# One DiT step on a Trainium2 core: half of the modulation moved from TensorE to VectorE multiply-adds

## The reference

```python
mod = silu(cond) @ w_mod + b_mod          # -> sh1, sc1, g1, sh2, sc2, g2, 2048 columns each
h = x * (1 + sc1) + sh1
z = h @ w_in                              # 8 neighbourhood heads (NA), latents of 8 MLA heads
o = concat(neighbourhood attention, latent attention) @ w_o
x = layernorm(ALPHA * x + g1 * o)
y = layernorm(ALPHA * x + g2 * swiglu(x * (1 + sc2) + sh2))
```

## Time and profile before

| | |
|---|---|
| median of 3 runs | 3181.38 us (3173.12 to 3184.36) |
| the profiled execution | 3185.31 us, span 3183.8 us, 43487 instructions |
| TensorE busy | 3027.6 us (95%), 16238 matmuls |
| weight loads | 2545.2 us (80%), beside the matmuls |
| VectorE busy | 1712.4 us (54%) |
| ScalarE busy | 1184.1 us (37%) |
| GpSimd busy | 168.1 us (5%) |
| split, VectorE L1202 | 239 recorded, 290.6 us, mean 1230 ns |
| split, ScalarE L752 | 239 recorded, 246.0 us, mean 1056 ns |
| load of a stream block | 503 of 512 KB, median 3.5 us from issue to landing |
| DMA over the span | 380 MB, 119 GB/s |

### The profile page before, as it was taken

The page is one execution under the profiler, slowest core; times in us unless marked ns, Lnnn a source line. Parts: engine busy times, 40 slices in busy tenths (PEclk is TensorE's granted clock), DMA queues, the critical chain, the costliest instruction groups (busy, mean ns, idle before and its releaser), DMA issues.

```text
span 3183.8 us, 43487 instructions
## 1 busy us (share of the span) xinstructions
PE 3027.6 (95%) x16238; PEld 2545.2 (80%) x16238; DVE 1712.4 (54%) x2513; ACT 1184.1 (37%) x1966; POOL 168.1 (5%) x203
## 2 busy tenths in 40 slices
PE   7899999999999999959999999999999999899997
PEld 2587676677766577849999999999999877687885
DVE  7626566551333432276666666666666534433348
ACT  7425555442433421164444444444444311212121
POOL 0200101000000010000000000000000000000004
PEclk9899999999989999969999999999999999999998
DMA  9836555641120131122222222222222423323232
GB/s 371 268 107 223 188 198 189 199 150 68 46 95 33 45 119 67 60 93 101 93 103 105 95 92 105 98 98 96 102 94 105 158 88 127 111 89 115 88 108 84
DMA packets 103745, 379.99 MB, mean 119 GB/s; under 512 B 13153, under 2 KB 13370, under 8 KB 102106
## 3 DMA queue, kind: packets, MB, share of 16 engines
q1 hardware_dynamic: 89088, 317.36, 28.0%
q0 software_dynamic: 13840, 61.02, 5.6%
q10 hardware_dynamic: 730, 0.38, 0.1%
HBM read 347.09 MB, written 35.31 MB: 120 GB/s over the span
## 4 chain that ended last, share of the span: by engine, by line
PE 82%; DVE 7%; DMA 5%; issue 3%; ACT 3%; SPq 0%; ACTq 0%; DVEq 0%; POOL 0%; POOLq 0%
PE ps L1682 13%; PE ps L1684 13%; PE ps L1683 13%; PE ps L2123 11%; PE ps L2125 11%; PE ps L2124 11%; DMA raw<-in_wstream 3%; PE ps L1853 2%; DVE wlo L1202 1%; DMA mraw<-in_wstream 1%; ACT whi L752 1%; PE ps L1805 1%; PE ps L1804 1%; PE ps L1826 1%; DVE mlo L1217 1%
## 5 line engine op out<-in xcount | busy, mean ns | idle before, releaser
L2123 PE MATMUL ps<-acth,ringh 128*128 128x320 f32 x2464 | 762.8, 310 | 17.4 <-DVE ringl L1507 17.4
L2124 PE MATMUL ps<-actl,ringh 128*128 128x320 f32 x2464 | 762.5, 309 | 0.0
L2125 PE MATMUL ps<-acth,ringl 128*128 128x320 f32 x2464 | 762.4, 309 | 0.0
L1202 DVE TENSOR_TENSOR wlo<-raw,whi 128x1024 fp32r<-128x1024 f32 x239 | 290.6, 1230 | 496.7 <-ACT whi L752 496.5
L2123 PEld LDWEIGHTS ps<-acth,ringh 128*128 128x128 f32 x2464 | 463.2, 188 | 17.8 <-DVE ringl L1507 17.8
L2124 PEld LDWEIGHTS ps<-actl,ringh 128*128 128x128 f32 x2464 | 463.2, 188 | 0.0
L2125 PEld LDWEIGHTS ps<-acth,ringl 128*128 128x128 f32 x2464 | 463.2, 188 | 0.0
L752 ACT ACTIVATE whi<-raw 128x1024 fp32r<-128x1024 f32 x239 | 246.0, 1056 | 402.0 <-PE ps L1684 374.7
L1682 PE MATMUL ps<-dwh,fring 128*128 128x512 f32 x820 | 327.3, 399 | 23.3 <-DVE dwl L1594 18.5
L1683 PE MATMUL ps<-dwl,fring 128*128 128x512 f32 x820 | 324.5, 396 | 0.0
L1684 PE MATMUL ps<-dwh,fring 128*128 128x512 f32 x820 | 324.5, 396 | 0.0
(11 more groups left out here) (294 smaller groups left out, 4907.0 us busy)
## 6 DMA issues: line engine op xcount, KB each, us to landing
raw<-in_wstream SPq DMA_DIRECT2D x503, 512.0 KB, 3.5
mraw<-in_wstream SPq DMA_DIRECT2D x64, 512.0 KB, 7.6
fscr<-fst POOLq DMA_DIRECT2D x44, 320.0 KB, 2.4
fst<-fscr SPq DMA_DIRECT2D x21, 640.0 KB, 4.1
acc<-in_xT SPq DMA_DIRECT2D x8, 640.0 KB, 18.8
oscr<-ost POOLq DMA_DIRECT2D x16, 320.0 KB, 2.5
acc<-in_xtok POOLq DMA_DIRECT2D x1, 5120.0 KB, 16.1
ostage<-oscr POOLq DMA_DIRECT2D x16, 320.0 KB, 3.9
```

The costliest lines, as they stand in the source:

```text
L1202: V.tensor_tensor(lo_of(n), raw[:, n % 4, :], hi_of(n).bitcast(f32), ALU.subtract).then_inc(lo_ready, 1)
L2123: mm(out, ringh[:, s, w], ah, start=first, stop=False, skip_group_check=True)
L2124: mm(out, ringh[:, s, w], al, start=False, stop=False, skip_group_check=True)
L2125: ins = mm(out, ringl[:, s, w], ah, start=False, stop=last, skip_group_check=True)
```

## The change

The first half of the modulation, and all that is not the modulation, computes what it did. The 128 blocks of the second half are no longer split and no longer go to TensorE. VectorE multiplies each by the conditioning as a per-partition scalar and adds it up, 128 x 512 at a time, for two rows and two halves of the block: four instructions. What is left is a sum over the 128 partitions, which TensorE does once per chunk, as rows (`row_sums`, for the gates) or as columns (`column_sums`, for shift2 and scale2). The gates get their bias on VectorE (`gate_row`), go to DRAM and are spread to 128 partitions by DMA.

```diff
+            def gemv(i, m, part=(0, 1)):
+                nb, u = MOD_SEQ.index(m), m // 8
+                s, b, buf = slot_of("m", m), m % 8, macc_of(u)
+                for kk in part:
+                    w = raw[:, s, kk * 512:(kk + 1) * 512]
...
+                    for c in range(2):
+                        if kk:
+                            dve.wait_ge(m_half, at(i, 8, 2 * nb + c + 1))
...
+                        v = buf[:, c, :]
...
+                            ins = V.scalar_tensor_tensor(out=v, in0=w, scalar=f, in1=v, op0=ALU.mult, op1=ALU.add)
...
+            def gate_row(u, bank):
+                dve.wait_ge(mred, reduces(u if u < 4 else u + 8))
+                dve.wait_ge(brow_in, 16 * (u + 1))
+                V.tensor_tensor(grow[:, :], ps[bank][0:2, :], grow[:, :], ALU.add).then_inc(grow_ready, 1)
...
+            def row_sums(u, bank):
+                pe.wait_ge(lo_ready, POS[("m", 8 * u + 7)] + 1)
+                mm(ps[bank][0:2, :], unit[:, 1:3], macc_of(u)[:, 0, :], start=True, stop=False)
+                mm(ps[bank][0:2, :], unit[:, 0:2], macc_of(u)[:, 1, :], start=False, stop=True).then_inc(mred, 1)
...
+            def column_sums(units, bank):
+                for n, u in enumerate(units):
...
+                    for j in range(4):
...
+                        mm(o, macc_of(u)[:, 0, w], unit[:, 1:3], start=True, stop=False)
+                        ins = mm(o, macc_of(u)[:, 1, w], unit[:, 0:2], start=False, stop=True)
```

The 128 blocks are placed over five stages instead of one:

```diff
+V_MODS = [0] * 4 + [1] * 8 + [2] * 4
+WO_MODS = [0 if b < 4 or b > 26 else 2 if 9 <= b < 18 else 1 for b in range(32)]
...
+    for h in range(NH):
+        order += [("m", 64 + 4 * h), ("m", 65 + 4 * h), ("w", B_HEAD + h + 2), ("m", 66 + 4 * h), ("m", 67 + 4 * h)]
```

That is 16 in the V projection, 32 in the NA stage (four per head, in halves between the softmax stages), 16 in the latent projections (one per block), 32 in the MLA heads (four per head) and 32 in the output projection (blocks 4 to 26). SyncE's loads are written out one by one in this order. In the NA stage and in the heads VectorE's queue becomes:

```diff
             def na_iter(i, stages):
+                for g in range(4):
+                    if stages:
+                        stage(i, -1, 2 * g, True, (1,))
+                        stage(i, -1, 2 * g, True, (0,))
+                    gemv(i, 32 + 8 * g, (0,))
+                    if g == 3:
+                        k_copy(at(i, 4, B_NA + 4), HT)
+                    split(i, B_NA + g + 2)
+                    if stages:
+                        stage(i, -1, 2 * g + 1, True, (1,))
+                        stage(i, -1, 2 * g + 1, True, (0,))
+                    elif g in (0, 3):
+                        gate_row(g // 3, 6 - g // 3)
+                    gemv(i, 32 + 8 * g, (1,))
...
                 if h < NH:
+                    if h == 0:
+                        dve.wait_ge(skv_out, 32)
+                    gemv(None, 64 + 4 * h)
+                    gemv(None, 65 + 4 * h)
 
                     dve.wait_ge(used, B_HEAD + h + 1)
                     V.tensor_copy(kT[:, 0:KEYS // 2], ps[0][:, 0:KEYS // 2]).then_inc(k_evac, 1)
                     for s in range(5):
                         stage(None, NH + h, s, False)
                         if s == 1:
-                            split(None, 0, B_HEAD + h + 2)
+                            split(None, B_HEAD + h + 2)
+                        if s in (2, 3):
+                            gemv(None, 64 + 4 * h + s)
```

On TensorE the feature block of the NA stage is cut in two (`outs=(0, 1)` and `(2, 3)`) with a `stage` call after each half. Row sums stand after V block 13, in the first NA head, after latent blocks 9 and 16 and four times in the output projection; column sums of shift2 in the first latent block, those of scale2 after block 0 of the output projection. Ahead of the NA loop TensorE waits for the second gate row:

```diff
             na_iter(None, False)
+
+            pe.wait_ge(grow_ready, 2)
+            pe.wait_ge(v_evac, 2 * TT)
             with pe.Fori(1, NH) as i:
...
+                if b == 0:
+                    column_sums(range(8, 12), 6)
+                if b in WO_ROWS:
+                    u = WO_ROWS.index(b)
+                    if u >= 2:
+                        pe.wait_ge(grow_ready, 3 + u)
+                    row_sums(12 + u, 4 + u % 2)
```

In the output projection VectorE's multiply-adds follow the split of each block, those of b = 7, 15 and 23 the evacuation of that block; GpSimd's queue gets the gate broadcast and the load of xs, which moves there from the first MLA head:

```diff
                 if k == 3:
-                    rows_in(rows2, D, 2 * D, rows2_in)
...
+                    pool.wait_ge(grow_out, 64)
+                    for c in range(2):
+                        pool.dma_start(gate[:, c, :], modg[c:c + 1, 0:D].to_broadcast([P, D])).then_inc(gate_in, 16)
+                if k == 8:
+                    pool.wait_ge(mred, reduces(11))
+                    pool.dma_start(xs, xtok).then_inc(xs_in, 16)
```

More of the change, by code:

```diff
@@ L485, in _, with stream_load @@
                 if g < 4:
[L486 to L494, removed]
+                    sp.dma_start(raw[:, g, :], wstream[stream_row(B_V + g)]).then_inc(loaded[g], 16)
+            def stream_load(p):
+                sp.wait_ge(lo_ready, p - 3)
+                sp.dma_start(raw[:, p % 4, :], wstream[stream_row(p)]).then_inc(loaded[p % 4], 16)
+            for p in range(B_V + 4, len(ORDER)):
+                stream_load(p)
             def gu_load(i, jj):
@@ L499, in gu_load @@
                         if q < 2:
-                            sp.wait_ge(lo_ready, B_FF - 2 + q)
+                            sp.wait_ge(lo_ready, max(p for p in range(len(ORDER)) if p % 4 == q) + 1)
                         if q == 2:
@@ L1259, in _ @@
                         h_rest(k)
-                        if b == 0 and 0 < k < 4:
-                            split(None, 0, B_V + k)
-                split(None, 0, B_V + b + 4)
+                        if b == 0 and k == 1:
+                            split(None, B_V + 1)
+                split(None, B_V + b + 2)
+                m = sum(V_MODS[:b])
+                for x in range(V_MODS[b]):
+                    gemv(None, m + x)
             def stage(i, a, s, na, parts=(0, 1)):
@@ L1466, in _ @@
                 if b < 30:
-                    split(None, 0, B_WO + b + 2)
-                if b == 24:
+                    split(None, B_WO + b + 2)
+                m = 96 + sum(WO_MODS[:b])
+                for x in range(WO_MODS[b]):
+                    gemv(None, m + x)
+                if b in WO_ROWS:
+                    gate_row(4 + WO_ROWS.index(b), 4 + WO_ROWS.index(b) % 2)
+                if b == 2:
                     mod2_parts()
@@ L1702, in tok_block, with feat_block @@
                 return ins
-            def feat_block(n, bh, bl, k0, first, last, before=None, after=None, widths=(HT, HT), banks=(0, 1, 2, 3), b2=None):
-                for o in range(4):
+            def feat_block(n, bh, bl, k0, first, last, before=None, after=None, widths=(HT, HT), banks=(0, 1, 2, 3), b2=None,
+                           outs=range(4)):
+                for o in outs:
                     if before:
@@ L1756, in _ @@
             turn_rows(None, 7)
-            def mod_columns(shift, scale, done):
-                for j in range(2 * KD):
-                    rows = shift if j < KD else scale
-                    ins = mm(ps[6][:, 2 * j:2 * j + 2], rows[:, j % KD * P:(j % KD + 1) * P], selt[:, 0:2],
-                             start=True, stop=True)
-                ins.then_inc(done, 1)
             for c in range(2):
```

449 lines of the change are left out of this document (240 added, 209 removed).

## The result

The changed kernel takes 3095.6 us (3082.4 to 3096.8, four runs) where the kernel before takes 3178.8: a ratio of 0.973, interval 0.970 to 0.976. The forecast was 3138 us. The kernel became faster, as forecast, and the heads behaved as told; the gain is 83 us instead of 43, about twice as large.

The account below looks back on a forecast made before the run. TensorE, busy in 95% of the span, was taken as the bound, stage by stage. From 3185.3 us: -4.5 - 7.6 - 7.1 - 120 + 17 + 80.5 + 6.7 - 8.2 = -43.2, less 3.9, gives 3138; range 3076 to 3172.

Parts of the forecast that it names:

- Heads: MLA heads: four multiply-add blocks each delay the kT copy, TensorE pauses and its clock falls; +80.5 us.
- The half clock: MLA heads: after the pause, scores and part of the PV product go at half clock; 7.5 us per head, seven times.
- The late kT: MLA heads: kT copy ends late behind multiply-adds, so TensorE stops for 3.5 us in each of eight heads.
- NA loop: Seven NA iterations: modulation products and idle time go, 58.4 to 41.3 us each; -120 us, bounds -127 and -100.
- meetings with GpSimd: NA loop: 1 us added per iteration, 40.3 to 41.3 us.
- rival C: NA iteration becomes bound by softmax and multiply-add chain; at 46 us it gives back 33, total 3171 us; chance 0.09.
- Latent stages: KV/q latents: column sums +12.2, two row sums +3.8, rotary part and v projection +1; together +17 us.
- Output projection: Gate broadcasts and mod_columns go, -23.5; column sums, row sums, late evacuations and queued loads are added; net +6.7 us.
- Down projection: Four gate2 broadcasts go, -13.7; the 2 MB DMA broadcast ahead of the x1 load adds +5.5; -8.2 us.
- Start, V projection, first NA head: Shorter constants wait -4.5, h parts ahead of splits -7.6, modulation products gone from first NA head -7.1 us.
- B: MLA heads: the clock stays up despite the pause; heads +28, total 3086 us; chance 0.25.
- D: VectorE: a multiply-add costs much more than 0.66 us, mainly in the heads; at 1.0 the total is 3206 us; chance 0.07.

Follow-up runs that it names:

- the pause filled: Changed kernel with ten extra unused TensorE products in heads 1 to 7, between the last transposition and the first scores: 3058.2 us, ratio 0.962.
- the blocks moved: Changed kernel with two of each head's four multiply-add blocks moved from ahead of the kT copy to behind it: 3033.6 us, ratio 0.954.
- The doubled kernel: Changed kernel with a second multiply-add, into a spare tile, beside each one of the NA stage: 3130.1 us, ratio 0.985.
- the schedule experiment: Changed kernel with no multiply-adds behind output-projection blocks 6, 14 and 22, two behind blocks 18 to 21 instead: 3079.8 us, ratio 0.969.

## Why the prediction was wrong in size, step by step

- **Heads, +80.5 forecast, +55.4 measured: the step that failed.** Mechanism, place and order of events were as told; what was added up was not. The experiments divide the 55.4. (1) The half clock: 275.6 in the kernel after less 237.7 with the pause filled is 37.9, where 7 x 7.5 = 52.5 was forecast. The clock fell after six of the seven pauses, at 6.3 us each in the mean; after the pause of 2.52 at 959.26 it stayed at 1.00, and the time to the next kT copy was 30.65, as with the pause filled. (2) The late kT: 237.7 less 213.6 with the blocks moved is 24.1, where 8 x 3.5 = 28 was forecast. Each of the seven was about as dear as forecast (3.4); the eighth does not exist, since eight copies have seven intervals. TensorE's pauses are 3.0 and 2.5 us in turn (every other head begins a new sum, whose first two instructions take 0.87 us together); the chain of VectorE's instructions from stage 2's maximum to the end of the copy took 17.1 and 16.5 us, where the prediction has 17.2. (3) Beside that the heads became 6.6 us shorter than before (213.6 against 220.3), through the first of them, a term that the prediction put at nothing without a word. Its own show what there was to gain: scores of 1.96 us at half clock at 896.09, after 0.92 of idle time. 37.9 + 24.1 - 6.6 = 55.4.
- **NA loop, -120 against -128.7.** Steps right but for the one us "for meetings with GpSimd", which is not there (40.07 against 40.3 without it); 7 x 1.23 = 8.6. A wrong working stood beside it: VectorE's load was put at 37 us by counting a maximum and a normalisation in all eight stages, where only five have them. The window says 26.74. The earlier trace rows would have given it: 35.71, less 16 splits of 1.22, plus four blocks of 2.7, is 27.0. The 37 made rival C seem near. The doubled kernel shows that C begins somewhere between 26.7 and 40.2 us of VectorE's work.
- **Latent stages, +17 against +12.5.** The price from the row was right: the 32 narrow products took 10.1 us and 1.9 more in products behind them at half clock, 12.0 for 12.2; two row sums about 2 each. What was missed is a gain of some 3.5 in the stages behind: the wait before the transpositions fell from 2.66 to 1.44, these ran warm (3.62 us instead of 4.50), and the distance of two full products fell from 0.2333 to 0.2290. ScalarE's copies of two successive tiles of six products in the kernel after:

```profile
716.88 0.60 ACT L1050 ACTIVATE vm<-ps 128x512 f32<-128x512 f32 x1 [0.77 <-PE ps L1803]
718.25 0.60 ACT L1050 ACTIVATE vm<-ps 128x512 f32<-128x512 f32 x1 [0.77 <-PE ps L1803]
```

  They are 1.37 apart; in the kernel before 1.40. In the output projection six take 1.40 in both kernels. The buffers lie at other addresses, but that this is the cause was not tried.
- **Output projection, +6.7 against +2.6.** The evacuations' lateness was priced at 10.8. TensorE's idle time at the chunk starts adds up to 7.6 us; counted by the distances of successive starts, the waits cost 9.8, against 1.3 in the kernel before. So 8.5 stand for the 10.8, and the schedule experiment confirms the place: 9.2 us. The other 2 us of this row are not assigned.
- **Down projection, -8.2 against -11.2.** The -13.7 for the four broadcasts is about right: four blocks took 41.63 us and now take 27.2 to 28.8. The +5.5 for 2 MB of DMA ahead of the loads is refuted, since the stage is as long without them ahead (654.8). The pause at this place did grow, from 1.98 to 8.28. Of these 6.3 us, 4.4 are the load of fst, which took 12.98 instead of 8.56 to land; 1.9 are TensorE's, which reached the wait 8.7 us after the load's issue instead of 10.6, no longer held up by the wait of 2.23. Why the load is slower stays open. The prediction counted the bytes, but did not look up which load TensorE waits for.
- **Start, V projection, first NA head:** -20.2 together against -19.2. The blocks of V came as the order of the h parts allows; this one was not tested by itself.
- **Rivals.** B (clock stays up, 3086) is nearest in number, yet it is not what happened: the clock fell after six of seven pauses. That its number came near is luck: its heads are 27 us too short, and the other terms, which it shares with the forecast, 21 too long. What spoke for it, that pauses of 1 us cost no clock, was wrong by the earlier trace rows, where the clock fell after one of 0.92. D (a dearer multiply-add) did not occur: 746 ns in the median, and 742 to 753 in all 120 of the heads. One of the 360 others took 2.62 us, beside an addition on GpSimd. The Trainium skill, "GPSIMD Engine Reference", section "8. Key points", says that the two engines share their way to SBUF and hinder each other where a VectorE instruction has two inputs there. This instance agrees: four multiply-adds, the long one among them, took 4.61 us instead of 2.73. VectorE's and GpSimd's timelines:

```profile
159.47 4.61 DVE L1288 SCALAR_TENSOR_TENSOR macc<-raw,conds,macc 128x512 f32<-128x512 f32 x4
```

```profile
160.95 2.57 POOL L679 TENSOR_TENSOR acc<-acc 128x896 f32<-128x896 f32 x1 [6.24 <-DMA acc<-tbl]
```

  In the sum, 250.4 us for 360 (overlaps left out), it does not matter here; GpSimd is busy for 5% of the span.
- **The range** (3076 to 3172) held the time, by the width given to B and to the heads, the terms that then decided.

## What to carry to other kernels

VectorE was idle for 62% of a head (10.44 of 27.4 busy), and work given to it was still not free where its queue was just then what another engine waited for: two of each head's four blocks cost 58 us in all ahead of a copy that TensorE needs, and nothing behind that copy. So for each added instruction name the next thing in its queue that another engine waits for, and put it right behind that, not ahead. A pause of TensorE can cost twice, once itself (24.1 us in the seven of these heads) and once in the half clock behind it (37.9); count both, count the intervals and not the heads, and look for pauses in the old kernel that the change may do away with.

## What the runs showed of the hardware

- **The same pause does not always bring the clock down.** In the kernel after, TensorE paused 2.49 us before 888.23 and fell to half clock within 1.1 us, and paused 2.52 before 961.78 and did not:

```profile
961.78 1.10 PE L1936 MATMUL ps<-kT,qT 128*128 128x512 f32 x2 [2.52 <-issue]
962.81 1.12 PE L1937 MATMUL ps<-krT,qrT 64*128 64x512 f32 x2
```

  The heads of one and the same order took 265 to 276 us in seven profiled executions, with pauses of nearly the same length. The first head shows the same with a shorter pause: TensorE, at a granted clock of 1.00, was idle for 0.70 and then for 0.92 us in both kernels. In the kernel before the scores at 896.09 took 1.96, at half clock; in the kernel after those at 759.64 took 1.13. So a forecast by "the clock falls" has a spread of some 10 us here, and what decides is not shown.
- **The clock can fall under products of two columns without any idle time.** From 533.9 on TensorE had nothing but narrow products, back to back; their distance (each is recorded as two) went from 0.22 to 0.43:

```profile
537.11 0.36 PE L1823 MATMUL ps<-unit,macc 128*128 128x2 f32 x2
537.34 0.36 PE L1822 MATMUL ps<-unit,macc 128*128 128x2 f32 x2
537.56 0.54 PE L1823 MATMUL ps<-unit,macc 128*128 128x2 f32 x2
537.96 0.57 PE L1822 MATMUL ps<-unit,macc 128*128 128x2 f32 x2
```

  The windows of the two stretches, busy throughout, at granted clocks of 1.00 and 0.52:

```profile
537.30:543.90 6.60, 6.60 (x34) 6.60 (x34) 0.00 (x0) 0.00 (x0) 0.00 (x0) 0.52 0.07 29
533.90:537.30 3.40, 3.40 (x33) 3.40 (x31) 0.30 (x1) 0.00 (x0) 0.82 (x1) 1.00 0.80 249
```
